# Moving columns of two groups of feed-forward matmuls walked in blocks of 16 or of 2

## What is computed

```python
FFN_HIDDEN = ((8 * D_MODEL + 3 * 256 - 1) // (3 * 256)) * 256   # 5632

def swiglu(h, w_gate, w_up, w_down):
    return (jax.nn.silu(h @ w_gate) * (h @ w_up)) @ w_down

for l in range(DEPTH):                                          # DEPTH = 2
    ...
    h = rms_norm(x, ffn_norm_g[l])
    x = x + swiglu(h, w_gate[l], w_up[l], w_down[l]).astype(x.dtype)
```

## Time and profile before

| | |
|---|---|
| median of 2 runs | 3421.03 us |
| the profiled execution, its own time | 3421.76 us |
| its span, first to last instruction | 3419.9 us |
| TensorE busy | 3412.1 us, 100% of the span |
| VectorE busy | 2041.3 us, 60% |
| ScalarE busy | 1674.0 us, 49% |
| DMA | 633.87 MB, 185 GB/s on average |
| TensorE clock granted | 1.000 of full speed, mean of the core |

### The profile page before, as it was taken

How to read it: one execution, slowest core, us unless ns; L and a number is a source line. 1 busy time by engine, 2 the same in 40 slices (tenths; PEclk the granted TensorE clock), 3 DMA queues, 4 the chain that set the end, 5 groups by cost and what they waited for, 6 DMA issues and landing times.

```text
span 3419.9 us, 40209 instructions
## 1 busy us (share of the span) xinstructions
PE 3412.1 (100%) x16716; PEld 2877.9 (84%) x16716; DVE 2041.3 (60%) x2138; ACT 1674.0 (49%) x1966; POOL 68.7 (2%) x84
## 2 busy tenths in 40 slices
PE   9999999999999999999999999999999999999999
PEld 8888888888888888888888888888888888888887
DVE  8767668455556877654444454578776544444444
ACT  5743464466555476564434333455756533333332
POOL 1000000000000020000000000000200000000000
PEclk9999999999999999999999999999999999999999
DMA  7453554554555544545555555555444455555554
GB/s 258 176 194 136 223 185 175 197 196 172 204 184 181 192 174 160 183 158 187 189 193 196 186 194 188 192 177 195 167 166 173 172 185 190 192 192 189 196 186 160
DMA packets 90646, 633.87 MB, mean 185 GB/s; under 512 B 10440, under 2 KB 10720, under 8 KB 16096
## 3 DMA queue, kind: packets, MB, share of 16 engines
q1 hardware_dynamic: 85536, 610.19, 49.7%
q0 software_dynamic: 4928, 21.11, 1.7%
HBM read 629.12 MB, written 2.14 MB: 185 GB/s over the span
## 4 chain that ended last, share of the span: by engine, by line
PE 98%; DVE 1%; DMA 1%; ACT 0%; issue 0%; SPq 0%; DVEq 0%; ACTq 0%
PE G L591 23%; PE G L593 23%; PE G L592 23%; PE G L603 12%; PE G L605 6%; PE M L970 2%; PE G L683 1%; PE G L685 1%; PE G L684 1%; PE M L1330 1%; PE G L583 0%; PE G L585 0%; PE G L584 0%; PE M L1485 0%; DMA w_raw<-in_s_lru 0%; PE M L1213 0%
## 5 line engine op out<-in xcount | busy, mean ns | idle before, releaser
L501 DVE TENSOR_TENSOR w_lo<-w_raw,w_hi 128x2048 fp32r<-128x2048 f32 x582 | 1323.7, 2276 | 1154.0 <-ACT w_hi L485 1152.3
L485 ACT ACTIVATE w_hi<-w_raw 128x2048 fp32r<-128x2048 f32 x582 | 1105.7, 1901 | 1427.1 <-PE G L593 1298.6
L591 PE MATMUL G<-w_hi,x_halves 128*128 128x512 f32 x1856 | 725.5, 391 | 0.0
L593 PE MATMUL G<-w_hi,x_halves 128*128 128x512 f32 x1856 | 722.5, 389 | 0.0
L592 PE MATMUL G<-w_lo,x_halves 128*128 128x512 f32 x1856 | 722.2, 389 | 0.0
L591 PE MATMUL G<-w_hi,y_halves 128*128 128x512 f32 x1640 | 644.9, 393 | 0.0
L593 PE MATMUL G<-w_hi,y_halves 128*128 128x512 f32 x1640 | 638.9, 390 | 0.0
L592 PE MATMUL G<-w_lo,y_halves 128*128 128x512 f32 x1640 | 638.3, 389 | 0.0
L603 PE MATMUL G<-x_halves,w_hi 128*128 128x512 f32 (+1 forms) x1392 | 440.8, 397 | 0.0
L593 PEld LDWEIGHTS G<-w_hi,x_halves 128*128 128x128 f32 x1856 | 348.4, 188 | 72.6
L592 PEld LDWEIGHTS G<-w_lo,x_halves 128*128 128x128 f32 x1856 | 348.6, 188 | 71.2
(11 more groups left out here) (486 smaller groups left out, 2551.9 us busy)
## 6 DMA issues: line engine op xcount, KB each, us to landing
w_raw<-in_s_up SPq DMA_DIRECT2D x176, 1024.0 KB, 4.8
w_raw<-in_s_down SPq DMA_DIRECT2D x88, 1024.0 KB, 4.8
w_raw<-in_s_ssd SPq DMA_DIRECT2D x40, 1024.0 KB, 4.8
w_raw<-in_s_hgrn SPq DMA_DIRECT2D x32, 1024.0 KB, 4.8
w_raw<-in_s_gate SPq DMA_DIRECT2D x32, 1024.0 KB, 4.8
w_raw<-in_s_mlstm SPq DMA_DIRECT2D x32, 1024.0 KB, 4.8
w_raw<-in_s_mlstm_gate SPq DMA_DIRECT2D x32, 1024.0 KB, 4.8
w_raw<-in_s_o_out SPq DMA_DIRECT2D x16, 1024.0 KB, 4.8
```

The source lines that it names most:

```text
L485: act.activation(whi[p % SETS][:, 0:n_], raw[p % RAW][:, 0:n_], ACT.Copy).then_inc(S("hi_ready"), 1)
L501: dve.tensor_tensor(wlo[p % RAW][:, 0:n_], raw[p % RAW][:, 0:n_], whi[p % SETS][:, 0:n_].bitcast(F32), ALU.subtract).then_inc(S("lo_ready" ...
L591: pe.matmul(o, ah[:, kk, tok], hi[:, k, :], start=first, stop=False)
L593: mm = pe.matmul(o, al[:, kk, tok], hi[:, k, :], start=False, stop=last)
```

## The change

A function `column_order` gives the moving operand and the output of the `tm` matmuls a new access pattern in two groups. In `up00` the 512 columns are seen as two halves of 256, each cut into 16 blocks of 16: the walk takes block 0 of the lower half, block 0 of the upper half, block 1 of the lower half, and so on. In `up01` the blocks have 2 columns, 128 in each half. Output and moving operand have the same order, so each product goes to the place where it went before. Every other group keeps its pattern.

```diff
+        def column_order(name, v):
+
+            if name == "up00":
+                return v.rearrange("p (half c x) -> p c half x", half=2, x=16)
+            if name == "up01":
+                return v.rearrange("p (half c x) -> p c half x", half=2, x=2)
+            return v
+
...
                             for t in range(NT):
                                 tok = slice(t * P, t * P + P)
-                                o = base[:, t, 0:w]
-                                pe.matmul(o, ah[:, kk, tok], hi[:, k, :], start=first, stop=False)
-                                pe.matmul(o, ah[:, kk, tok], lo[:, k, :], start=False, stop=False)
-                                mm = pe.matmul(o, al[:, kk, tok], hi[:, k, :], start=False, stop=last)
+                                o, w_hi, w_lo = (column_order(name, v) for v in (base[:, t, 0:w], hi[:, k, :], lo[:, k, :]))
+                                pe.matmul(o, ah[:, kk, tok], w_hi, start=first, stop=False)
+                                pe.matmul(o, ah[:, kk, tok], w_lo, start=False, stop=False)
+                                mm = pe.matmul(o, al[:, kk, tok], w_hi, start=False, stop=last)
```

## The result

The changed kernel takes 3515.74 us (median of 2 runs) against 3421.03 us: 94.7 us more, a ratio of 1.0277 with a 95% interval from 1.026 to 1.0294. The direction and the range of the prediction held; its size, 164 us, was too large by 69 us.

What follows compares the result with a forecast made beforehand. TensorE was taken as the bound, so longer matmul turns reach the end one for one. 0 us for `up00` plus 163.9 us for `up01` gave 3585 us as a median, 4.8% slower, with a range of 3416 to 3620 us.

Steps and rivals of the forecast that it cites:

- What bounds the kernel: Whole kernel: TensorE is the bound, busy 3412.1 of 3419.9 us, so a matmul's turn goes to the end one for one.
- Blocks of 16: 0 us: `up00`: blocks of 16 still take 4 float32 from each stretch before moving, 1.67 ns each as now, so 0 us.
- a bound of 20 us: `up00`: if each change of block cost one stretch-opening of 0.83 ns, 32 x 0.83 x 768 = 20 us.
- Blocks of 2: 256 openings at 1.67 ns, 163.9 us: `up01`: 256 openings of 4-float32 stretches take 426.8 ns instead of 213.4 a matmul, 163.9 us over 768.
- two signs of being wrong: Forecast wrong if blocks of 2 turn under 316 ns; reasoning by stretches wrong if blocks of 16 cost as much.
- Nothing to be gained: Both groups: columns already pass one per clock, so no gain from address order; a vanished fixed part would give 20 us, 0.6%.
- the fixed part of a turn: In each 226.7 ns matmul turn, the 13.3 ns left after 512 columns at 0.417 ns.
- No change: Rival: TensorE gets columns at 0.417 ns in any order with runs of two or more; 3421 us, chance 0.36.
- Both groups pay: Rival: the jump or PSUM addition in another order costs at any block length; 3749 us doubled, 3519 at 1.3 times; chance 0.12.
- A part of the price: Rival: blocks of 2 cost less than double, as some openings overlap; 82 us at 1.5 times, 16 at a tenth; chance 0.15.
- L2002's ratio of 1.81: VectorE row with output and mask at every second element, 1336 against 738 ns; would give 141 us, 3562 us.
- VectorE's free runs of 2: VectorE at scan level 2 (L2024), every second run of 2 float32: 1219 against 1225 ns in order, so jumping costs nothing.

Runs made afterwards that it cites:

- the woven kernel: Kernel before, with every moving weight row read as single elements alternating between its halves and weights laid out in HBM to suit: 3300.00 us, ratio 0.9647.
- `up11` with fresh sums: Group walking in blocks of 2 between halves as in the changed kernel, each matmul opening its sum anew instead of adding to the bank: 340.0, then 333.3 ns.
- round 4 quarters: Blocks going round four quarters of the columns: output alone in blocks of 2, 226.7 ns; moving operand alone in blocks of 4, 268.0 ns.
- halves 4: Output and moving operand of one group walk in blocks of 4 alternating between the two halves, against order of address: 250.0 ns a turn.
- halves 2: Walk in blocks of 2 alternating between the two halves, as `up01` in the changed kernel: 340.0, then 333.3 or 333.4 ns a turn.
- the last two sets: Two kernels against the one before, six moving-operand walks each, testing lanes: turns of 215.8 to 486.7 ns, then 215.8 to 237.0 ns.

## Why the prediction came out as it did

**What bounds the kernel.** Right. The turn of a matmul went to the end one for one: 10.1 + 84.5 us in the two stretches, 94.7 in all, and 120.9 gained where the turn fell. Clock, waits and the other groups (226.7 ns) stayed as said.

**Blocks of 16: 0 us.** Measured 10.3 us. I gave the price of a jump a bound of 20 us and took nothing, since a block of 16 uses every stretch fully. (The bound had a slip: it called 0.83 ns the price of an opening, where my own count had 1.67 ns; with that it is 41 us. The runs give 13.3 ns for 32 blocks, 0.42 ns each.) The block lengths show that even full use leaves 17 ns a turn for blocks of 8 and 23 for blocks of 4; a jump has a small price of its own, which is not explained.

**Blocks of 2: 256 openings at 1.67 ns, 163.9 us.** Measured 84.6 us. This is the term that was mis-sized. The premise, that new stretches can't be opened faster than the walk in order opens them, gave 440 ns a turn, and walks in which nothing is used again soon took 443 to 493. But the walk of the change comes back to each stretch after one jump, and that takes 333 to 340 (327 in two other walks of the kind). I had counted each visit as a new opening, though the walk was written in the diff: 0 and 1, 256 and 257, then 2 and 3 from the same 16 bytes. And the premise itself was wrong in its form, so that its nearness to the 443 ns is luck: by 1.67 ns an opening, every fourth element would take 512 x 1.67 + 13.3 = 868 ns, and it took 460 to 461. The count that fits most walks is by lane, though no run shows a lane: in order, each lane uses a stretch twice and pays 11 ns; in blocks of 2 it uses it once, leaves, and comes back. Neither of the two signs of being wrong that I had set was met (a turn under 316 ns; blocks of 16 as dear as blocks of 2), so they were too coarse to show this.

**Nothing to be gained.** I had written "the order of addresses gives no reason for a gain": that was the step, with 20 us as the bound in these 1536 matmuls. For this change that held, for the place it did not: 11.0 of the 13.3 ns that I called the fixed part of a turn were a price of reading in order. I subtracted them without asking what they were, and the faster kernel lay there. Nor are they fixed: with 256 columns (L587 to L589 of the woven kernel) the weave takes the turn from 119.8 to 111.7 ns, 8 ns (46 turns in 5.51 us before and in 5.14 us woven). The Trainium skill had the clue, which I left unused: "TensorE: Matmul & The Clock Gate", section "Wait — 56ns, not 53.3ns?", gives N / 2.4 GHz and about 2.5 ns from start to start, 215.7 ns for 512 columns. The woven walk takes 215.8, and the 226.7 of the walk in order is 11 ns more than this rule. With 256 columns the rule's figures give an estimate of 109.2 ns, and the woven walk's 111.7 is 2.5 ns above it.

**The rivals.** No change is refuted (ratio 1.0277). Both groups pay is right in that blocks of 16 pay too, but 10.3 us and not in proportion; the second of its causes, the addition in PSUM, is refuted by the outputs that walked alone and by `up11` with fresh sums. A part of the price is what happened: at 1.5 times, 82 us, it named 84.6 us almost exactly, with the reason "some openings overlap", and I gave it 0.15. But 1.5 was one point picked on a scale that went down to a tenth, and no run shows overlapping openings, so the nearness of the number is luck. So is that of the 3519 us of "both groups pay" at 1.3 times: it lies 3 us from the measured time with 49 us in each group, where the groups took 10.1 and 84.5. L2002's ratio of 1.81 and VectorE's free runs of 2 bracketed the result (1.47 to 1.50), and neither decided anything. L2002 was also misread as a price of gaps: at level 1 of the scan L2024 takes single elements at every second place in the same 1.22 us.

**The rules of the Trainium skill.** "Advanced Engine Details and Errata", section Memory Cachelines, on PSUM: an access pattern that is not contiguous slows matmuls significantly. These runs show 226.7 ns for outputs in blocks of 2 and of 16, between halves, round 4 quarters and round 64 parts, so on writing pairs the sentence doesn't hold; they agree with the other sentence, that every two consecutive elements should be contiguous. Single elements on the writing side were not tried. On SBUF: lines of 16 bytes, and at least two hits on a line for full speed. The runs agree with the 16 bytes (shifting blocks of 4 by 8 bytes, 250.0 to 330 ns), but for TensorE two hits on end are neither needed (single elements woven between halves take 215.8 ns) nor enough for the fastest turn. Counted by lane, one hit at a time costs 57 ns a turn or more (283.3 to 493.3), and even two on end cost 11.

## What to carry to other kernels

Where a dense stream of 512-column float32r matmuls bounds a kernel, look at the order in which the moving operand is read, and not at that of the output, as long as the output is written in pairs at least. Columns 0, 4, 1, 5, 2, 6, 3, 7 and so on, with the data laid out to suit, take 215.8 ns a turn where the order of address takes 226.7. That is 4.8% of a turn, for a new access pattern and a change of layout in HBM. This weave within 8 columns was run in one group, with weights that were not laid out for it; in a whole kernel only the weave of the two halves was run. Blocks of 2 whose stretch isn't used on end, and blocks of 4 that are not aligned to 16 bytes, cost 1.4 to 2.2 times the turn in order. And when a turn is split into columns and a fixed part, measure what the fixed part is made of before taking it as given.

## What was not expected of the hardware

A moving operand whose columns all come from one address still takes 216.3 ns. No walk that was tried goes below 215.8 ns, and reading in order misses that by 11 ns. Single elements at steps of 3 and 4 cost 450 to 461 ns, about as much as pairs at every other place (451 to 453): two columns per visit were worth hardly more than one.

Three things stay open. The small price of a jump at full use of the stretches (250.0 ns for halves 4, 268.0 round 4 quarters, 231.1 for every other block of 4). The turn of halves 2, which is 340.0 ns up to the transposes inside a group's fifth chunk and 333.3 behind them, in five groups of four kernels alike and also with streams 1024 apart, but 327.2 throughout when the streams are 260 apart, and 326.7 when they are 8 apart. And the lanes themselves, which are a reading of turns: of the 12 walks of the last two sets 10 came out as expected, one 3 ns above its range and one (283.3 ns) well below, but nothing in the trace shows a lane. Nor do the lanes explain every walk before: shifted blocks of 8 take 348 ns and shifted blocks of 4 only 330, though a lane changes its stretch less often in the former, and the walk in order shifted by 8 bytes takes 233 ns, though each lane still uses a stretch twice.
